# The eight modulation chunks of GpSimd moved to the weights' ring and TensorE

## Chip, cores and metric
The kernel runs on one core of one Trainium2 chip. The metric is the device time of one execution in microseconds (us).

## What is computed
Two blocks of two transformer layers each, on one sequence of 256 tokens of 1024 channels, all in float32. The first block's layers are modulated by a condition vector `c`; cut to what matters here:

```python
# first block, for each of 2 layers
mod = silu(c) @ ada_w[l] + ada_b[l]        # 1024 x 6144 weights, six vectors of 1024
sh_m, sc_m, gt_m, sh_f, sc_f, gt_f = split(mod, 6)
h = rms_norm(x, norm_mix) * (1 + sc_m) + sh_m
# o_a windowed attention, o_b compressed/selected attention, o_c gated delta net, all from h @ w_in
x = x + gt_m * (concatenate([o_a, o_b, o_c]) @ w_out)
h = rms_norm(x, norm_ffn) * (1 + sc_f) + sh_f
x = x + gt_f * ((silu(gate) * up) @ w_down)     # gate, up = h @ w_gate_up
```

The modulation vector of a layer is computed in 12 chunks of 512 columns, m = 0 to 11 for the first layer and 12 to 23 for the second. A chunk's weights are 1024 x 512, 2 MB. The second block (block attention with a learned choice of keys, dilated attention, and feed-forward layers with a short convolution) has no modulation. It uses a table of relative-position biases that the kernel widens in DRAM first (`bias_wide`, 6 MB).

## The kernel before
**Stages.** For each layer of the first block: `in` (five chunks of columns and one of tokens), `tok`, `cmp` (the compression network), attention, the gated delta net, `out` (two chunks), `gu` (gate and up, eleven chunks) and `dn` (down, eight tiles of 128 output channels). Layer numbers are added: gu0, dn0, gu1, dn1. Then the second block with `even`, `tail`, `o0`, `up0`, `down0`, `odd`, `o1`, `up1`, `down1`.

**Weights' ring.** All weights come through one ring of three slots (`SLOTS`). The order of the chunks is fixed when the program is built, by `phase` and `ada_chunks` (lines 98 to 122). SyncE (SP) issues the loads in that order; a load waits until the chunk three places ahead of it in the ring has been used (`load`, line 488): for weights of a matmul until TensorE has finished with it (`gemm_ready`), for an ada chunk until its sums have been copied out (`acc_ready`). SP runs its instructions in order, so a load that waits holds up everything behind it.

**Splitting.** A float32 product is made of three fp32r matmuls: high part by high, high by low, low by high. Each chunk is split in two halves. ScalarE copies a half to its high part (`high`, line 1111, a 2048-column copy, 1408 columns for down), and VectorE subtracts to get the low part (`low`, line 1483); GpSimd does this subtraction for the first three halves of `out` (line 1959). High parts are kept for three halves (`AHEAD`), so `high(u)` waits for TensorE to be done with half `u - 3`, and for a first half also for the chunk's landing.

**Modulation on TensorE.** 16 of the 24 chunks go through the ring. `ada_dots` (line 694) multiplies the chunk by silu(c) with eight 512-column matmuls into four row groups; ScalarE copies the rows out (`ada_rows`, line 1131); `modulations` (line 704) sums the four groups with four one-column matmuls into columns of PSUM bank 7. Chunks 0 to 3 come at the very start, 4 and 5 (16 and 17 in layer 1) inside `in`, the next two around `cmp` and attention, and two more in the delta net at inverse levels 1 and 3.

**Modulation on GpSimd.** The other eight, m = 10 to 15, 22 and 23, are loaded by GpSimd's own DMA queue into a part of the arena once the last mixer output is ready (`mix_ready`), multiplied by silu(c) and added up there (`weigh`, line 1967: one operation of 4096 columns, two of 2048 or 1024, one of 512). TensorE adds the partitions with the same `modulations`, ahead of gu and within it, and, for 12 to 15, ahead of tiles 1, 3, 5 and 7 of dn0. The modulations of m = 12 to 15 are read by VectorE in the last step of dn0's residual (line 1698).

**Delta net.** The inverse of a triangular matrix is built in seven levels. In a level TensorE makes T1 (line 821) for two halves of the heads, ScalarE copies each (line 1222), TensorE makes the two products dx (lines 829 and 831), VectorE updates X and XT (lines 1666 and 1668). GpSimd prepares the next level's mask (line 1993). ScalarE splits the first two halves of `out` ahead of level 1, the third after level 6 (`late_high`).

**End of a stage.** `norm_squares` (line 1080) squares the residual tile pairs as VectorE finishes them, with the `high` copies for the next stage in between; `norm_sums` sums on TensorE (line 690); ScalarE takes the root (line 1096), then one `high`, then `norm_high` writes the high part of the normalised tiles.

## Time and profile before

| | us |
|---|---|
| median of 3 timed runs | 1814.04 |
| lowest and highest | 1806.9, 1814.69 |
| profiled execution, own time | 1805.96 |
| its span from the first to the last instruction | 1804.2 |
| TensorE (PE) busy | 1608.9 |
| VectorE (DVE) busy | 1044.7 |
| ScalarE (ACT) busy | 784.3 |
| GpSimd (POOL) busy | 280.8 |
| mean granted TensorE clock, of full speed | 0.933 |

Busy times are unions of an engine's instructions and overlap between engines. Waits are inferred from semaphore events. PEclk is the granted TensorE clock as a share of the higher of its two levels, 2.4 GHz. Times inside the trace count from the span's start.

### The profile page before, as it was taken

The page shows a single profiled execution, that of the slowest core. Times are in us where ns is not written, and L with a number is a line of the kernel's source. Part 1 is how long each engine was busy: PE and PEld are TensorE (multiplying, and loading weights), DVE is VectorE, ACT ScalarE, POOL GpSimd, SP SyncE. Part 2 cuts the span into 40 slices and gives each one's busy share as a digit, 9 for nine tenths or more (in the row PEclk, how much of TensorE's full clock was granted, in tenths as well). Part 3 has the DMA queues.
Part 4 walks back from the last instruction along what each step waited for, and adds up shares of the span by engine and source line. Part 5 has one row for each costly group of instructions (what it writes and reads, how often), then busy time and mean ns, then how long its engine had stood idle before and what let it go on. Part 6 is the DMA issues. An engine that isn't in the chain of part 4 may idle for free.

```text
span 1804.2 us, 29358 instructions
## 1 busy us (share of the span) xinstructions
PE 1608.9 (89%) x12322; PEld 1510.8 (84%) x12322; DVE 1044.7 (58%) x1393; ACT 784.3 (43%) x1175; POOL 280.8 (16%) x102
## 2 busy tenths in 40 slices
PE   5899788899989997888999899569999998899997
PEld 2888478899988884788999799448999988789997
DVE  1573545886664735458554633685876454567853
ACT  3344423444343434234443443354664444556642
POOL 0000246663510002366000000220000000200000
PEclk7997799899999977998999899789999999999999
DMA  8365522565552551225544734202553545045442
GB/s 364 135 230 227 174 94 98 216 245 192 187 205 99 226 208 54 94 94 187 186 158 161 266 141 154 93 1 94 187 186 129 205 157 187 6 143 184 167 161 88
DMA packets 30191, 287.82 MB, mean 160 GB/s; under 512 B 2887, under 2 KB 11367, under 8 KB 11784
## 3 DMA queue, kind: packets, MB, share of 16 engines
q1 hardware_dynamic: 28888, 269.51, 40.7%
q0 software_dynamic: 1152, 16.78, 2.4%
q8 instruction: 79, 1.29, 0.3%
q14 instruction: 24, 0.20, 0.0%
q10 hardware_dynamic: 48, 0.05, 0.0%
HBM read 285.23 MB, written 7.39 MB: 162 GB/s over the span
## 4 chain that ended last, share of the span: by engine, by line
PE 73%; DVE 16%; ACT 3%; DMA 3%; issue 3%; POOL 1%; SPq 0%; POOLq 0%; DVEq 0%; ACTq 0%
PE bank L610 20%; PE bank L611 19%; PE bank L612 19%; DVE w_lo L1490 4%; DMA ring<-w_mix 2%; PE bank L992 2%; PE bank L690 2%; PE bank L748 2%; DVE arena L1804 2%; PE bank L831 1%; PE bank L736 1%; DVE lg L1516 1%; DVE h L1881 1%; PE bank L829 1%; ACT w_hi L1124 1%
## 5 line engine op out<-in xcount | busy, mean ns | idle before, releaser
L610 PE MATMUL bank<-hi_T,w_hi 128*128 128x256 f32 x2312 | 669.8, 290 | 35.1 <-DVE h_lo L1473 16.4
L612 PE MATMUL bank<-hi_T,w_lo 128*128 128x256 f32 x2312 | 664.3, 287 | 0.0
L1490 DVE TENSOR_TENSOR w_lo<-ring,w_hi 128x2048 fp32r<-128x2048 f32 (+2 forms) x218 | 508.9, 2345 | 228.7 <-ACT w_hi L1124 227.4
L611 PE MATMUL bank<-h_lo,w_hi 128*128 128x256 f32 x2056 | 590.8, 287 | 0.0
L1124 ACT ACTIVATE w_hi<-ring 128x2048 fp32r<-128x2048 f32 (+3 forms) x226 | 391.8, 1735 | 353.3 <-PE bank L612 280.3
L610 PEld LDWEIGHTS bank<-hi_T,w_hi 128*128 128x128 f32 x2312 | 455.2, 197 | 41.2 <-issue 33.1
L612 PEld LDWEIGHTS bank<-hi_T,w_lo 128*128 128x128 f32 x2312 | 454.6, 197 | 0.0
L611 PEld LDWEIGHTS bank<-h_lo,w_hi 128*128 128x128 f32 x2056 | 404.3, 197 | 0.4
L610 PE MATMUL bank<-act_hi,w_hi 128*128 128x256 f32 x704 | 201.5, 286 | 9.4 <-DVE act_lo L1503 7.7
L611 PE MATMUL bank<-act_lo,w_hi 128*128 128x256 f32 x704 | 200.5, 285 | 0.0
L612 PE MATMUL bank<-act_hi,w_lo 128*128 128x256 f32 x704 | 200.4, 285 | 0.0
L1953 POOL TENSOR_TENSOR lg<-lg,rec 128x512 f32<-128x512 f32 (+2 forms) x32 | 43.0, 1342 | 775.3 <-DVE rec L1532 734.0
L610 PEld LDWEIGHTS bank<-act_hi,w_hi 128*128 128x128 f32 x704 | 136.5, 194 | 10.3 <-DVE act_lo L1503 8.3
L611 PEld LDWEIGHTS bank<-act_lo,w_hi 128*128 128x128 f32 x704 | 136.6, 194 | 0.0
L612 PEld LDWEIGHTS bank<-act_hi,w_lo 128*128 128x128 f32 x704 | 136.4, 194 | 0.0
L1141 ACT ACTIVATE arena<-bank 128x256 f32<-128x256 f32 (+3 forms) x99 | 39.1, 405 | 152.0 <-PE bank L612 152.0
L1916 DVE SCALAR_TENSOR_TENSOR arena<-bank,v,arena 128x254 f32<-128x254 f32 (+1 forms) x176 | 72.9, 476 | 38.0 <-ACT arena L1426 37.8
L1964 POOL TENSOR_TENSOR w_lo<-ring,w_hi 128x2048 fp32r<-128x2048 f32 x8 | 36.0, 4531 | 298.9 <-ACT w_hi L1124 298.9
L1973 POOL TENSOR_TENSOR arena<-arena 128x2048 f32<-128x2048 f32 (+1 forms) x16 | 80.2, 5014 | 1.3
L1971 POOL TENSOR_TENSOR arena<-arena,c_silu 128x4096 f32<-128x4096 f32 x8 | 63.5, 7938 | 71.4 <-DMA arena<-ada 71.4
L611 PE MATMUL bank<-mix_lo,w_hi 128*128 128x256 f32 x256 | 73.9, 289 | 0.0
L610 PE MATMUL bank<-w_hi,hi_T 128*128 128x256 f32 (+2 forms) x240 | 68.1, 284 | 6.5 <-DVE w_lo L1490 6.5
(217 smaller groups left out, 2053.0 us busy)
## 6 DMA issues: line engine op xcount, KB each, us to landing
ring<-w_gu SPq DMA_DIRECT2D x22, 2048.0 KB, 8.2
ring<-w_dn SPq DMA_DIRECT2D x32, 1408.0 KB, 5.9
ring<-w_up SPq DMA_DIRECT2D x22, 2048.0 KB, 7.8
ring<-ada SPq DMA_DIRECT2D x16, 2048.0 KB, 7.4
ring<-w_mix SPq DMA_DIRECT2D x12, 2048.0 KB, 8.1
arena<-ada POOLq DMA_DIRECT2D x8, 2048.0 KB, 8.9
ring<-even_in SPq DMA_DIRECT2D x8, 2048.0 KB, 8.2
ring<-odd_in SPq DMA_DIRECT2D x6, 2048.0 KB, 7.8
```

Source lines behind the costliest of these rows:

```text
L610: nc.tensor.matmul(out, wh, xh, start=start, stop=False)
L611: nc.tensor.matmul(out, wh, xl, start=False, stop=False)
L612: return nc.tensor.matmul(out, wl, xh, start=False, stop=stop)
L690: last = nc.tensor.matmul(bank[:, 7, 0:S], const("ones"), h[:, k, :], start=(k == 0), stop=(k == KT - 1))
L748: last = nc.tensor.matmul(bank[0:HD, 6, lo * P:hi * P], v(kt), pT[0:n, u % 2, kt, lo * P:hi * P], start=U["start"] and kt == 0, stop=U["en ...
L1124: nc.scalar.activation(w_hi[:, u % AHEAD, 0:size], ring[:, slot, part * size:(part + 1) * size], ACT.Copy)\
L1141: nc.scalar.activation(dst, src, func).then_inc(gemm_freed, 1)
L1490: V.tensor_tensor(w_lo[:, n % SLOTS, at], ring[:, n % SLOTS, at], w_hi[:, u % AHEAD, 0:size].bitcast(F32), ALU.subtract).then_inc(w_lo_rea ...
L1916: V.scalar_tensor_tensor(out=cv[:, b, half, shift:S], in0=bank[:, 2 * b + half, 0:S - shift], scalar=cw[:, tap, at], in1=cv[:, b, half, sh ...
L1953: ins = G.tensor_tensor(out, out, along(rec[:, b, :], w), ALU.mult)
L1971: ch(G.tensor_tensor(ada_late, ada_late, along(c_silu, CH), ALU.mult))
L1973: ch(G.tensor_tensor(ada_late[:, 0:half], ada_late[:, 0:half], ada_late[:, half:2 * half], ALU.add))
```

## The change
All 24 chunks go through the ring and TensorE. In each layer six ada chunks instead of four stand between `cmp` and `out` in the ring, and the delta net takes one at each of the levels 1, 2, 3 and 4. The four for layer 1's start (12 to 15) come in dn0 behind tiles 0, 2, 4 and 6, dots and all; their modulations run between the tiles, the last one behind the last tile. ScalarE's row copies stand in `norm_squares` for dn0 between two `high` copies. The three `late_high` copies of `out` stand behind levels 3, 4 and 5. `weigh`, its buffers and its semaphore go. What follows is the diff, cut to its core.

```diff
-    NEXT_ADA = (1, 3, 5, 7)
+    NEXT_ADA = (0, 2, 4, 6)
...
         phase(f"cmp{l}", ["compress"] * 2)
-        ada_chunks(4)
+        ada_chunks(6)
         phase(f"out{l}", OUT)
         phase(f"gu{l}", UP)
-        phase(f"dn{l}", DOWN, FT * P // 2)
+        phase(f"dn{l}", DOWN, FT * P // 2, ada_after=() if l else NEXT_ADA)
...
# SyncE
                 load_phase(f"cmp{l}", w_cmp[l], 0, full)
-                for j in range(2, 6):
+                for j in range(2, 8):
                     load_ada(m + j)
                 if l == 0:
                     sp.dma_start(v2[:, :, :], vec2).then_inc(vec2_in, 16)
...
-                load_phase(f"dn{l}", w_dn[l], 2, FT * P)
+                for j, at in enumerate(phases[f"dn{l}"]["at"]):
+                    load(at, w_dn[l][j], FT * P)
+                    if l == 0 and j in NEXT_ADA:
+                        load_ada(ADA_L + NEXT_ADA.index(j))
...
# TensorE, delta_net
                 for lv in range(LEVELS):
-                    if lv == 3:
-                        modulations(m_next, m_next + 1)
+                    if lv in (3, 4):
+                        modulations(m_next + lv - 3, m_next + lv - 2)
                     pe.wait_ge(mb_ready, l * LEVELS + lv + 1)
-                    if lv in (1, 3):
-                        ada_dots(m_next + lv // 2)
+                    if 1 <= lv <= 4:
+                        pe.wait_ge(acc_ready, m_next + lv - 1)
+                        ada_dots(m_next + lv - 1)
...
-                modulations(m_next + 1, m_next + 2)
+                modulations(m_next + 2, m_next + 4)
...
# TensorE, down
-                    if name == "dn0" and j in NEXT_ADA:
-                        m = ADA_L + NEXT_ADA.index(j)
-                        if m == ADA_L:
-                            pe.wait_ge(mod_read, 2)
-                        modulations(m, m + 1)
...
                         last.then_inc(gemm_ready, 1)
+                    if name == "dn0" and j in NEXT_ADA:
+                        m = ADA_L + NEXT_ADA.index(j)
+                        if m == ADA_L:
+                            pe.wait_ge(mod_read, 2)
+                        else:
+                            modulations(m - 1, m)
+                        ada_dots(m)
+                if name == "dn0":
+                    modulations(ADA_L + ADA_FIRST - 1, ADA_L + ADA_FIRST)
...
# ScalarE, norm_squares
-                        for u in ahead if j < 3 else ahead[:-1]:
+                        for u in ahead[:-1]:
                             high(u)
+                        if norm_input[n] == "dn0":
+                            ada_rows(ADA_L + j)
+                        if j < 3:
+                            high(ahead[-1])
...
# ScalarE, delta_net
-                act.wait_ge(mb_ready, l * LEVELS + 1)
-                late_high(l, 0, 2)
                 for lv in range(1, LEVELS):
...
-                    if lv in (1, 3):
-                        ada_rows(m_next + lv // 2)
-                late_high(l, 2, AHEAD)
+                    if lv <= 4:
+                        ada_rows(m_next + lv - 1)
+                    if lv >= 3 and lv < 3 + AHEAD:
+                        late_high(l, lv - 3, lv - 2)
...
# GpSimd
-            def weigh(m):
-
-                pool.dma_start(ada_late, ada[m].rearrange("p (k n) -> p k n", k=KT)).then_inc(late_in, 16)
-                pool.wait_ge(late_in, 16 * (ada_alone.index(m) + 1))
-                ch(G.tensor_tensor(ada_late, ada_late, along(c_silu, CH), ALU.mult))
-                for half in (KT // 2, KT // 4):
-                    ch(G.tensor_tensor(ada_late[:, 0:half], ada_late[:, 0:half], ada_late[:, half:2 * half], ALU.add))
-                pool.wait_ge(mod_ready, m - 1)
-                G.tensor_tensor(late_sums[:, m % 2, :], ada_late[:, 0, :], ada_late[:, 1, :], ALU.add).then_inc(acc_ready, 1)
-                pool.wait_ge(acc_ready, m + 1)
```

The modulations ahead of gu and within it go as well (in the loop over layers and in `up`).

## Rows read from the trace of the kernel before

**Rows 1.** the page: busy us, share, instructions by engine; then the chain's shares.
```profile
PE 1608.9 (89%) x12322; PEld 1510.8 (84%) x12322; DVE 1044.7 (58%) x1393; ACT 784.3 (43%) x1175; POOL 280.8 (16%) x102
...
PE 73%; DVE 16%; ACT 3%; DMA 3%; issue 3%; POOL 1%; SPq 0%; POOLq 0%; DVEq 0%; ACTq 0%
```

**Rows 2.** timeline, out0: start, us, engine, line, operands, count, [idle before].
```profile
297.54 7.01 POOL L1971 TENSOR_TENSOR arena<-arena,c_silu 128x4096 f32<-128x4096 f32 x1 [7.52 <-DMA arena<-ada]
...
298.54 8.16 DVE L1490 TENSOR_TENSOR w_lo<-ring,w_hi 128x2048 fp32r<-128x2048 f32 x1 [1.46 <-ACT w_hi L1124]
...
329.22 2.29 DVE L1490 TENSOR_TENSOR w_lo<-ring,w_hi 128x2048 fp32r<-128x2048 f32 x1
```

**Rows 3.** timeline: norm sums and root after out0; norm sums after o0.
```profile
313.68 2.75 PE L690 MATMUL bank<-h,cn 128*128 128x256 f32 x12
...
320.59 0.47 ACT L1096 ACTIVATE std<-bank,cn 128x256 f32<-128x256 f32 x1 [1.41 <-PE bank L690]
...
1241.70 3.61 PE L690 MATMUL bank<-h,cn 128*128 128x256 f32 x16
```

**Rows 4.** timeline of the inverse levels, layer 0: ScalarE's copies, TensorE's ada work.
```profile
237.29 0.60 ACT L1222 ACTIVATE arena<-bank 128x512 f32<-128x512 f32 x1 [1.80 <-PE bank L821]
...
238.68 0.59 ACT L1136 ACTIVATE arena<-bank 128x512 f32<-128x512 f32 x1
...
242.71 0.60 ACT L1222 ACTIVATE arena<-bank 128x512 f32<-128x512 f32 x1 [3.44 <-PE bank L821]
...
251.66 0.60 ACT L1222 ACTIVATE arena<-bank 128x512 f32<-128x512 f32 x1 [6.71 <-PE bank L821]
...
257.07 0.60 ACT L1222 ACTIVATE arena<-bank 128x512 f32<-128x512 f32 x1 [3.44 <-PE bank L821]
...
263.19 0.60 ACT L1222 ACTIVATE arena<-bank 128x512 f32<-128x512 f32 x1 [3.87 <-PE bank L821]
...
269.30 0.60 ACT L1222 ACTIVATE arena<-bank 128x512 f32<-128x512 f32 x1 [3.87 <-PE bank L821]
...
247.73 0.95 PE L714 MATMUL bank<-cn,arena 128*128 128x1 f32 x8
...
248.61 1.92 PE L700 MATMUL bank<-ring,c_wide 128*32 128x512 f32 x16
```

**Rows 5.** DMA issues, 168 to 210 (last: landing time); stretch 178 to 203.
```profile
bias_wide<-bias_dram SPq DMA_DIRECT2D x1, 6144.0 KB, 31.9
...
ring<-w_out SPq DMA_DIRECT2D x1, 2048.0 KB, 28.5
...
178.00:203.00 25.00, 19.77 (x94) 11.88 (x94) 18.68 (x34) 13.22 (x55) 5.80 (x8) 0.80 0.95 300
```

**Rows 6.** stretches: length, busy us (count) by engine, clock, DMA share, GB/s.
```profile
339.10:458.95 119.85, 117.14 (x969) 116.19 (x968) 94.71 (x49) 52.10 (x52) 65.63 (x17) 1.00 0.58 217
...
837.30:953.26 115.96, 115.96 (x969) 115.95 (x968) 66.59 (x51) 52.14 (x52) 11.71 (x3) 1.00 0.47 170
...
458.95:532.36 73.41, 68.84 (x561) 68.46 (x561) 43.37 (x30) 25.35 (x20) 24.78 (x7) 0.98 0.55 205
...
953.26:1016.69 63.43, 63.43 (x529) 63.39 (x528) 28.35 (x25) 25.25 (x20) 0.00 (x0) 1.00 0.56 204
```

**Rows 7.** a stretch shortly after dn0's first wait.
```profile
466.80:470.20 3.40, 3.40 (x18) 3.40 (x18) 0.00 (x0) 0.00 (x0) 0.00 (x0) 0.50 0.00 0
```

**Rows 8.** the page's DMA issues: count, KB each, median us from issue to landing.
```profile
ring<-w_dn SPq DMA_DIRECT2D x32, 1408.0 KB, 5.9
...
ring<-ada SPq DMA_DIRECT2D x16, 2048.0 KB, 7.4
```

**Rows 9.** timeline at the turn from gu1 to dn1.
```profile
953.32 1.38 ACT L1124 ACTIVATE w_hi<-ring 128x1408 fp32r<-128x1408 f32 x1 [2.56 <-PE bank L612]
...
956.28 0.68 DVE L1503 TENSOR_TENSOR act_lo<-arena,act_hi 128x512 fp32r<-128x512 f32 x1
```

**Rows 10.** timeline: ScalarE's first normalised tiles of in1.
```profile
538.74 1.30 ACT L1108 ACTIVATE hi_T<-h,mod 128x256 fp32r<-128x256 f32 x3 [0.61 <-DVE h L1455]
```

More of the change, by code:

```diff
@@ L117, in ada_chunks @@
         for _ in range(n):
-            if late_ada(len(ada_at)):
-                ada_at.extend([None] * (2 + ADA_FIRST))
             ada_at.append(count["chunk"])
@@ L122, in ada_chunks @@
             count["chunk"] += 1
-    def late_ada(m):
-        return ADA_L - 2 <= m < ADA_L + ADA_FIRST or m >= ADA - 2
-    NEXT_ADA = (1, 3, 5, 7)
+    NEXT_ADA = (0, 2, 4, 6)
     IN_ADA = (2, 4)
@@ L148, in hybrid_then_mixture @@
     phase("down1", DOWN, FT * P // 2)
-    ada_at.extend([None] * 2)
-    ada_alone = [m for m in range(ADA) if ada_at[m] is None]
-    on_pe = [m for m in range(ADA) if ada_at[m] is not None]
     def ada_bank(m):
         i = m % ADA_L
-        return i + 2 if i < ADA_FIRST else 2 if i == ADA_FIRST + 2 else 6
+        return i + 2 * (m < ADA_L) if i < ADA_FIRST else 2 if i == ADA_FIRST + 2 else 6
     late = [u for l in range(L1) for u in range(phases[f"out{l}"]["u0"], phases[f"out{l}"]["u0"] + AHEAD)]
@@ L189, in hybrid_then_mixture @@
         c_in = sb("c_in", [P, KT])
-        c_silu = sb("c_silu", [P, KT])
         c_wide = sb("c_wide", [P, KT, 32])
@@ L273, in hybrid_then_mixture @@
         acc = view(18432, 2, CH)
-        ada_late = view(19008, KT, CH)
-        late_sums = pT[:, :, 0, :]
         qk2 = view(0, 25, S)
@@ L323, in hybrid_then_mixture @@
         mod_ready = sem("mod_ready")
-        late_in = sem("late_in")
         mod_read = sem("mod_read")
@@ L709, in modulations @@
                         at = MOD_COL + 4 * m + t
-                        if ada_at[m] is not None:
-                            sums_m, ones = acc[:, m % 2, :], const("pick")[:, 0:1]
-                        else:
-                            sums_m, ones = late_sums[:, m % 2, :], const("ones")[:, 0:1]
-                        last = nc.tensor.matmul(bank[:, 7, at:at + 1], sums_m[:, t * P:t * P + P], ones,
-                                                start=True, stop=True)
+                        last = nc.tensor.matmul(bank[:, 7, at:at + 1], acc[:, m % 2, t * P:t * P + P],
+                                                const("pick")[:, 0:1], start=True, stop=True)
                     last.then_inc(mod_ready, 1)
@@ L873, in projection, with up @@
                     columns_chunk(name, nn, 4 * nn, (hi_T, mix_lo), ready)
-            def up(name, first, m_next=None):
+            def up(name, first):
                 ph = phases[name]
@@ L897, in up @@
                 for j in range(SLOTS * turns, 11):
-                    if m_next and j == SLOTS * turns:
-                        modulations(m_next, m_next + 1)
                     one(j, u0 + 2 * j + 1, t0 + 4 * j - 3)
@@ L1016, in _ @@
                 pe.wait_ge(std_ready, n + 2)
-                modulations(m + 6, m + 7)
-                up(f"gu{l}", norm_end[n + 1] - KT, m + 7)
+                up(f"gu{l}", norm_end[n + 1] - KT)
                 down(f"dn{l}", 11 * (l + 1))
@@ L1131, in ada_rows @@
             def ada_rows(m):
-                act.wait_ge(rows_ready, on_pe.index(m) + 1)
+                act.wait_ge(rows_ready, m + 1)
                 if m >= 2:
@@ L1264, in _ @@
             act.wait_ge(c_loaded, 16)
-            nc.scalar.activation(c_wide[:, :, :], along(c_in[:, :], 32), ACT.Silu)
-            nc.scalar.activation(c_silu[:, :], c_in[:, :], ACT.Silu).then_inc(c_ready, 1)
+            nc.scalar.activation(c_wide[:, :, :], along(c_in[:, :], 32), ACT.Silu).then_inc(c_ready, 1)
             act.wait_ge(tab_ready, 1)
@@ L1965, in low @@
                                 ALU.subtract).then_inc(w_lo_ready, 1)
-            def weigh(m):
-                pool.dma_start(ada_late, ada[m].rearrange("p (k n) -> p k n", k=KT)).then_inc(late_in, 16)
-                pool.wait_ge(late_in, 16 * (ada_alone.index(m) + 1))
-                ch(G.tensor_tensor(ada_late, ada_late, along(c_silu, CH), ALU.mult))
-                for half in (KT // 2, KT // 4):
-                    ch(G.tensor_tensor(ada_late[:, 0:half], ada_late[:, 0:half], ada_late[:, half:2 * half], ALU.add))
-                pool.wait_ge(mod_ready, m - 1)
-                G.tensor_tensor(late_sums[:, m % 2, :], ada_late[:, 0, :], ada_late[:, 1, :], ALU.add).then_inc(acc_ready, 1)
-                pool.wait_ge(acc_ready, m + 1)
-            pool.wait_ge(c_ready, 1)
             for l in range(L1):
@@ L1996, in _ @@
                     low(u)
-                pool.wait_ge(mix_ready, 3 * (l + 1))
-                for m in ada_alone[(2 + ADA_FIRST) * l:(2 + ADA_FIRST) * (l + 1)]:
-                    weigh(m)
             pool.wait_ge(w_lo_ready, phases["o0"]["u0"] + 1)
```

## The prediction
> **What bounds the kernel now.** I read the engine shares and the chain first. TensorE is busy 89% of the span and holds 73% of the chain, so time is won where TensorE waits and lost where it gets more to do or waits anew; GpSimd's 281 us matter only through what they hold up [rows 1]. What they hold up shows on VectorE's rows at the end of out0: one half-chunk subtraction (`low`) takes 8.16 us there against 2.29 us later. It began 1 us after GpSimd's first weighing multiplication (297.54 to 304.55) and ended at 306.70, one plain duration after it [rows 2]. Then I read TensorE's stretches by stage, the inverse levels on ScalarE's copies, and last the landing times of the SP queue, since the change moves loads.
>
> The sum is made against the profiled execution (span 1804.2, own time 1805.96 us). The three timed runs have the median 1814.04, 8 us above it.
>
> **Gains: the weighing goes.**
> (a) End of out0: TensorE starts the norm sums at 313.68, but the last four wait for squares that wait for stretched `low`s, and the standard deviation is taken at 320.59. Where no GpSimd work is near, 16 such matmuls run on in 3.61 us [rows 3]. So std would come at 313.7+3.6 = 317.3: 3.3 us saved. Layer 1 shows the same picture once, 3.0 us. Together -6.3.
> (b) gu0 against gu1, ten chunks each between the same issues: 119.85 and 115.96 us [rows 6]. The difference is waits behind stretched DVE work: -3.9. Each of the two stretches also holds one modulation (four one-column matmuls and their weight loads, 0.95 us as a group, some 0.8 once the pipeline overlaps) which moves into the delta net: -1.6. Together -5.5.
> (c) The modulation before gu goes too; it lay in the wait for the normalised tiles, so 0. GpSimd's own DMA queue goes; nobody waited on it but GpSimd: 0.
>
> **Costs in the inverse levels, both layers.** ScalarE's first T1 copy marks each level: 237.29, 242.71, 251.66, 257.07, 263.19, 269.30 [rows 4]. A plain level is 6.1 us. Dots and a modulation ahead of level 3 make that step 8.95, and the next is 5.4, because both halves are then ready. So dots with modulation cost 2.85-0.7 = 2.1, and dots alone (1.92 us on TensorE) 1.2. The change adds dots at level 2 and dots with modulation at level 4: +3.35 a layer. ScalarE's row copies (0.6) and the `late_high` of 1.9 after levels 3, 4, 5 fit in its gaps as long as the chunk is there. The second modulation after the output matmuls (0.8) lies in the wait for `on_ready`; uncovered it would cost 0.8 a layer.
>
> **The load that ends up in the way (layer 0).** SP is one queue in program order. Today `bias_wide` (6 MB, DRAM to DRAM) is issued after the ada load that waits for the sums of m = 6, in the attention stage. In the new order two more ada loads stand ahead of it, and the last, m = 11, waits for the sums of m = 8: ScalarE's copy at 238.68 to 239.27, inside level 1 [rows 4]. So `bias_wide` goes out at about 240, and w_out's first chunk, which now waits for the sums of m = 9 (level 2, about 246.5), behind it. What such a place in the queue costs is on record: the w_out chunk issued behind `bias_wide` today needed 28.5 us to land, and the 16 DMA engines moved 300 GB/s for the 25 us in which that copy ran (178 to 203) [rows 5]. Harmless there: the levels only begin after 230, and nothing on ScalarE waits for it before. Now: ada 11 issued 239.3, landed +7.4 = 246.7 [rows 8]; `bias_wide` 25 us, to 271.7; w_out's own 2 MB at least 5 us more (7.4 less the start), 277.1. But `late_high(l, 0, 1)` stands in ScalarE's program after level 3, ahead of the T1 copies of level 4, and it waits for that chunk. Queued behind it on ScalarE: T1 copies of level 4, sums of m = 11, all that follows; TensorE waits for the copies. Copy of the half 1.9: level 4's T1 copy at 279.1 instead of 261.1; level 5 +5.4, level 6 +6.1 = 290.6 against 269.30 now: +21.3. TensorE stands still some 16 us before; after a wait of 2.8 us it was granted half its clock (0.50, the 1.2 GHz level) for a stretch [rows 7], and the dx matmuls are what a level consists of, so I add 3 (bounds 0 and 7). Layer 0: +24.3. Bounds from the rows: if the bias copy did not hold w_out at all, +3.35; if w_out needed its full 28.5 us after the bias issue plus ada 11, 4 more than taken. I take the middle mechanism because the 28.5 us row is this very pair of transfers. Layer 1 has no such copy: +3.35.
>
> The Trainium skill bears on this ("DMA: Bandwidth & Descriptors", Queues, rings and completion order): on each DMA engine the descriptors of one issuing queue are consumed in ring order. By that rule w_out waits out the whole bias copy, total about +30; if instead transfers of one queue shared the engines evenly, w_out would land near 262, and the total would be about +11. The trace's 28.5 us agree with the rule.
> For (a) and (b), "SBUF — State Buffer", Who interferes with whom, says that a DVE operation with two SBUF inputs is shut out for the whole of a GpSimd instruction that reads SBUF; the 8.16 us row agrees, and without GpSimd the whole stretch is returned. No other sum comes from it.
>
> **dn0.** Undisturbed, dn1 takes 63.43 us; dn0 takes 73.41 now, with four modulations, a 2.8 us wait for act_lo, and others [rows 6]. New: 63.43 + four dots of 1.9 (7.5) + three modulations between tiles (2.5) = 73.4, so the work alone makes up for what goes. Then the ring. (i) ada 12 takes the slot after w0, so w1 waits for gu's last chunk (t = 0), lands at +5.9 [rows 8], and ScalarE's gate chunk 10 has `high` of w1's first half ahead of `hidden_high(10)`. In dn1 these steps run at +0.06 to +3.70 (`high` starts 953.32, act_lo ends 956.96, last issue 953.26) [rows 9]; all start 5.9 later: act_lo at +9.6, while TensorE wants it at half a tile, +3.96. Wait 5.6, and half clock after it, 2. (bounds 0 and 3.4.) (ii) w3, w5, w7 wait for the odd tile before (T), with an ada load issued at T-1.9 (ScalarE's rows copy comes after `high` of the same half). Landed: T-1.9+7.4+3.3 = T+8.8, `high` 1.38, `low` 1.6: T+11.8; TensorE is there at T+7.9+0.8+1.9 = T+10.6. Wait 1.2, three times: 3.6 (bounds 0 and 9). dn0 = 73.4+5.6+2+3.6 = 84.6: +11.2.
>
> **dn0 to in1.** The last modulation comes after the last tile and after ScalarE's row copy, and VectorE's `modulation(1)` and gain, then the last residual, behind it: about +2.1 on std. Then `high(ahead[-1])` needs in1's second chunk; its load waits for the sums of m = 15 (end of dn0 +0.5), lands +7.4, copy 1.9: +9.8, and `norm_high` stands behind it on ScalarE. Now hi_T starts at 538.74, 6.4 after dn0's end at 532.36 [rows 10]. The two overlap: +3.4 in all (bounds 2.1 and 4.5).
>
> **Sum.** -6.3 -5.5 +24.3 +3.35 +11.2 +3.4 = +30. On the profiled execution 1836, on the median 1844; as the timed runs spread from 1806.9 to 1814.7, I forecast 1842.
>
> **Rivals.**
> 1. The bias copy does not hold w_out (shares the engines evenly). For it: 300 GB/s is a mean over 25 us, and w_out's packets may well slip in between. Against: the 28.5 us. Then layer 0 costs about 5 instead of 24: +11, 1825. Chance 0.10.
> 2. Not slower: loads are hidden everywhere. w_out's chunk lands before level 4's copies want it, w1 within 4 us of gu's end, in1's second chunk before std. It decides at one point, whether SP gets past ada 11 and the bias copy before level 3 ends (about 255). Then only -6.3-5.5+3.35+3.35+0 (dn0) +1.4 (last modulation) = -3.7: 1810. For it: DMA runs at 0.5 to 0.6 of its time in gu and dn. Against: the order on SP. Chance 0.08.
> 3. Waits feed the clock: after the 16 us stand TensorE stays at the low level into the solve (+7), dn0's odd tiles wait 3 instead of 1.2 (+5), +42: 1856. For it: every idle stretch here is followed by PEclk 0.5. Against: levels keep TensorE busy otherwise. Chance 0.12.
> The forecast has 0.70.
>
> Range for 8 in 10: 1820 to 1857, from rival 1 to rival 3; the forecast's own range is 1832 to 1852. What one can tell from no change is about 0.5% (9 us). Slower by more: forecast, rival 3, and half of rival 1: 0.87. Within: half of rival 1 and most of rival 2: 0.10. Faster: 0.03.
>
> **What the new profile would show.** Right: a wait of ScalarE's `w_hi` copy for DMA of w_out of 15 to 22 us in layer 0 and none in layer 1; GpSimd's busy time far below 281 us; `low` at 2.29 in out0; ada dots about level 2 and 4; a wait for act_lo of 5 to 6 us at dn0's start; hi_T of in1 about 10 us after dn0. Wrong: bias_wide landing before 250, or level 4's copies at 261; gu0 still slower than gu1; dn0 at 74.

## The result and the profile after

| | us, median (range), runs |
|---|---|
| before | 1812.49 (1806.90 to 1814.69), 4 |
| after | 1839.22 (1832.64 to 1840.31), 4 |
| ratio | 1.0145, 95% interval 1.0111 to 1.0179 |

The kernel became 26.7 us slower between the medians; the forecast was 1842, 28 to 30 us slower. The profiled execution took 1839.05 us with a span of 1837.3, which is 33.1 us more than the span before (the execution profiled before was a low one of its runs, the one profiled now is not). The comparison of traces below is against these 33.1.

The page after, in the form of [rows 1]: busy time and the chain's shares.

```profile
PE 1629.5 (89%) x12450; PEld 1519.1 (83%) x12450; DVE 965.4 (53%) x1393; ACT 787.0 (43%) x1182; POOL 113.3 (6%) x62
...
PE 75%; DVE 12%; DMA 7%; ACT 3%; issue 2%; POOL 1%; POOLq 0%; SPq 0%; DVEq 0%; ACTq 0%
```

GpSimd lost 167.5 us of work and VectorE 79 us of stretching, as the change meant. TensorE gained 20.6 us. What ate the gain stands in the chain: DMA went from 3% to 7% of it. A shift at a time, measured between the same events of both traces (start of the group named to start of the next; the end of level 0 is taken at TensorE's first T1 product of layer 0 and at ScalarE's first T1 copy of level 1 in layer 1):

| stretch | forecast, us | measured, us |
|---|---|---|
| start to the end of level 0, layer 0 | 0 | +0.4 |
| inverse levels and what follows, to out0's first product | +24.3 | +23.8 |
| out0 to its root | -3.3 | -2.3 |
| gu0, to dn0's first product | -4.7 | -5.9 |
| dn0 and the turn to in1's first `hi_T` | +14.6 | +19.7 |
| in1 to the end of level 0, layer 1 | 0 | -1.9 |
| inverse levels of layer 1 | +3.35 | +3.65 |
| out1 to its root | -3.0 | -3.3 |
| gu1, dn1 | -0.8 | -1.4 |
| the rest | 0 | +0.4 |
| sum | +30.4 | +33.1 |

**Levels of layer 0.** ScalarE's timeline over the levels (L1211 copies T1, L1115 splits a weight, L1127 copies an ada chunk's rows); compare [rows 4].

```profile
238.90 0.60 ACT L1211 ACTIVATE arena<-bank 128x512 f32<-128x512 f32 x1 [12.56 <-PE bank L807]
...
246.37 0.60 ACT L1211 ACTIVATE arena<-bank 128x512 f32<-128x512 f32 x1 [5.49 <-PE bank L807]
...
254.62 0.60 ACT L1211 ACTIVATE arena<-bank 128x512 f32<-128x512 f32 x1 [6.28 <-PE bank L807]
...
277.80 1.91 ACT L1115 ACTIVATE w_hi<-ring 128x2048 fp32r<-128x2048 f32 x1 [21.20 <-DMA ring<-w_out]
279.62 1.07 ACT L1211 ACTIVATE arena<-bank 128x512 f32<-128x512 f32 x2
...
287.22 0.60 ACT L1211 ACTIVATE arena<-bank 128x512 f32<-128x512 f32 x1 [4.25 <-PE bank L807]
...
293.33 0.60 ACT L1211 ACTIVATE arena<-bank 128x512 f32<-128x512 f32 x1 [2.07 <-PE bank L807]
```

Between levels 3 and 4 lie 25.0 us where there were 5.4, and the bracket names the reason: the split of out0's first half, which stands in ScalarE's program between the two, waited 21.20 us for its load. The T1 copies of level 4 were queued behind it. SP's queue shows why the load was late (start, time taken at the queue, the load issued), and the DMA views how long it took (KB each, median us from issue to landing; the copy from the view of 235 to 290, out0's first load alone from the view of 248 to 250):

```profile
168.37 72.86 SPq L479 DMA_DIRECT2D ring<-ada  x4
...
241.75 0.62 SPq L535 DMA_DIRECT2D bias_wide<-bias_dram  x1
248.37 13.91 SPq L479 DMA_DIRECT2D ring<-w_out  x2
```

```profile
bias_wide<-bias_dram SPq DMA_DIRECT2D x1, 6144.0 KB, 31.1
ring<-w_out SPq DMA_DIRECT2D x1, 2048.0 KB, 29.4
```

SP passed the last ada load at 241.2 and sent the 6 MB copy at 241.75 (about 240 in the forecast). w_out went out at 248.37 behind it and was there at 277.8 (277.1 in the forecast), 4.9 us after the copy (241.75 + 31.1 = 272.9). In the kernel before, the load behind the copy also landed 4.9 us after it (203.5 and 208.4, [rows 5] with the issue times 171.59 and 179.91). TensorE stood still for 16.5 us:

```profile
PE bank L815 <- ACT arena L1211: 16.5, 1, 16.5
```

The step from level 4 to level 5, which begins at a granted clock of 0.50, took 7.6 us where experiment 1 below has 5.4. Another 1.2 us of the +23.8 lie before level 1's copies: from 231.5 to 237.5 the mean clock was 0.72, against 1.00 in the kernel before. Experiment 1 has the same 0.72 there and the three runs of experiment 5, with the same program up to there, have 1.00, so these 1.2 us are no price of the change.

**out0.** `low` beside no GpSimd work is 2.29 us, where [rows 2] has 8.16, and the sixteen norm sums run on as one group, as after o0. The rows are VectorE's, TensorE's and ScalarE's of one stretch of the timeline; compare [rows 3].

```profile
323.69 2.29 DVE L1479 TENSOR_TENSOR w_lo<-ring,w_hi 128x2048 fp32r<-128x2048 f32 x1 [1.46 <-ACT w_hi L1115]
...
338.82 3.61 PE L679 MATMUL bank<-h,cn 128*128 128x256 f32 x16
...
342.48 0.47 ACT L1087 ACTIVATE std<-bank,cn 128x256 f32<-128x256 f32 x1 [2.31 <-PE bank L679]
```

**Stretches.** Windows by length, busy us (count) of PE, PEld, DVE, ACT, POOL, granted clock, DMA share and GB/s, as [rows 6]: gu0, dn0, gu1 of the changed kernel, then two stretches at a clock of 0.50, behind the end of the levels and in dn0, as [rows 7].

```profile
359.93:474.96 115.03, 115.03 (x961) 115.03 (x960) 58.90 (x50) 52.03 (x52) 0.00 (x0) 1.00 0.48 177
474.96:566.45 91.49, 79.28 (x619) 73.03 (x617) 28.62 (x25) 26.57 (x24) 0.00 (x0) 0.93 0.54 205
870.96:986.01 115.05, 115.05 (x961) 115.05 (x960) 58.92 (x50) 52.02 (x52) 0.00 (x0) 1.00 0.47 171
...
312.20:319.03 6.83, 5.95 (x28) 5.95 (x29) 1.27 (x4) 0.10 (x1) 0.00 (x0) 0.50 0.00 0
482.90:486.30 3.40, 1.74 (x8) 1.75 (x9) 1.68 (x3) 1.13 (x1) 0.00 (x0) 0.50 0.00 0
```

gu0 now equals gu1, TensorE busy without a gap, 4.8 us shorter than before; gu1 is 0.9 shorter, which is its one modulation. dn0 went from 73.41 to 91.49, of which TensorE stood still 12.2 us (4.6 before). What it waited for in 470 to 570 (us in total, times, longest):

```profile
PE bank L599 <- DVE w_lo L1479: 6.5, 3, 2.6
PE bank L599 <- DVE act_lo L1492: 5.7, 1, 5.7
```

and how the first of the odd tiles' waits comes about, on TensorE (dots L689) and ScalarE:

```profile
490.95 1.92 PE L689 MATMUL bank<-ring,c_wide 128*32 128x512 f32 x16
...
513.98 0.55 PE L599 MATMUL bank<-act_hi,w_hi 128*128 128x256 f32 x1 [2.44 <-DVE w_lo L1479]
...
499.45 0.57 ACT L1127 ACTIVATE arena<-bank 128x512 f32<-128x512 f32 x1
510.80 1.38 ACT L1115 ACTIVATE w_hi<-ring 128x1408 fp32r<-128x1408 f32 x1 [10.78 <-DMA ring<-w_dn]
```

The dots end at 492.87, but ScalarE copies their rows at 499.45, behind the third of the splits that it makes ahead. The next ada load waits for that copy and goes out at 500.05, one us before the load of w3, so that both are under way at once: 9.8 us from issue to split, where the page has a median of 5.8 for w_dn. The loads of w5 and w7 went out 2.1 us behind an ada load and took 8.8 and 9.9.

### The profile page after: what moved, and what is told of

Read it like the earlier page. It is cut to its first block, busy times and chain, and to the rows that moved or that the text cites. A ratio compares the mean times of both kernels' runs of the same rounds, so it can differ in the third digit from the quotient of the medians.

```text
span 1837.3 us, 29587 instructions
## 1 busy us (share of the span) xinstructions
PE 1629.5 (89%) x12450; PEld 1519.1 (83%) x12450; DVE 965.4 (53%) x1393; ACT 787.0 (43%) x1182; POOL 113.3 (6%) x62
## 4 chain that ended last, share of the span: by engine, by line
PE 75%; DVE 12%; DMA 7%; ACT 3%; issue 2%; POOL 1%; POOLq 0%; SPq 0%; DVEq 0%; ACTq 0%
PE bank L599 20%; PE bank L600 20%; PE bank L601 20%; DMA ring<-w_mix 2%; PE bank L980 2%; PE bank L679 2%; DMA ring<-w_dn 2%; PE bank L733 2%; DMA ring<-w_out 2%; PE bank L689 2%; DVE arena L1793 1%; DVE w_lo L1479 1%; PE bank L817 1%; PE bank L721 1%; PE bank L807 1%
## 5 line engine op out<-in xcount | busy, mean ns | idle before, releaser
L1479 DVE TENSOR_TENSOR w_lo<-ring,w_hi 128x2048 fp32r<-128x2048 f32 (+2 forms) x218 | 447.7, 2062 | 295.9 <-ACT w_hi L1115 294.4
L1115 ACT ACTIVATE w_hi<-ring 128x2048 fp32r<-128x2048 f32 (+3 forms) x226 | 391.7, 1734 | 399.8 <-PE bank L601 263.4
L599 PEld LDWEIGHTS bank<-act_hi,w_hi 128*128 128x128 f32 x704 | 138.2, 196 | 21.2 <-DVE act_lo L1492 11.2
L600 PE MATMUL bank<-w_lo,hi_T 128*128 128x256 f32 (+2 forms) x240 | 68.3, 285 | 0.0
L601 PE MATMUL bank<-w_hi,h_lo 128*128 128x256 f32 (+2 forms) x240 | 68.3, 284 | 0.0
L689 PE MATMUL bank<-ring,c_wide 128*32 128x512 f32 x384 | 57.7, 727 | 9.3 <-DMA ring<-ada 8.9
```

The lines of the kernel that those rows point to most:

```text
L599: nc.tensor.matmul(out, wh, xh, start=start, stop=False)
L600: nc.tensor.matmul(out, wh, xl, start=False, stop=False)
L601: return nc.tensor.matmul(out, wl, xh, start=False, stop=stop)
L689: last = nc.tensor.matmul(bank[rows, ada_bank(m), :], c_wide[:, k, :], w[:, k, :], start=k < 4, stop=k >= 4, tile_position=(0, 32 * (k % 4)))
L1115: nc.scalar.activation(w_hi[:, u % AHEAD, 0:size], ring[:, slot, part * size:(part + 1) * size], ACT.Copy)\
L1479: V.tensor_tensor(w_lo[:, n % SLOTS, at], ring[:, n % SLOTS, at], w_hi[:, u % AHEAD, 0:size].bitcast(F32), ALU.subtract).then_inc(w_lo_rea ...
```

## Experiments

Each kernel is the changed one with the edit shown. Ratios are to the kernel before, on the same chip, with the 95% interval. The kernel before had a median of 1811.17 beside experiments 1 to 4, of 1809.58 beside experiment 5 and the run "early rows, last early", and of 1812.74 beside the other runs of experiment 6 and "again". So a difference between runs of different groups is given by the medians and, where it matters, by the ratios too.

### 1. The bias copy ahead of the added loads

```diff
-                for j in range(2, 8):
+                for j in range(2, 6):
                     load_ada(m + j)
...  # v2 and bias_wide, layer 0
+                for j in range(6, 8):
+                    load_ada(m + j)
```

> The copy of bias_wide is issued ahead of the two ring loads that the change added (modulations 6 and 7 of layer 0), not behind them. Theory: the layer-0 levels grew by 23.8 us because the copy now lies ahead of w_out in its DMA queue, so that ScalarE's split of w_out waits 21.2 us; the dots, splits and transposes themselves cost about what they cost in layer 1 (3.65 us). Then the split of w_out waits for nothing long, the levels of layer 0 take about 3.5 us more than in the kernel before, and the time falls by 20 us, to about 1819. Rival, that the growth of layer 0's levels is the added work of the engines (the copies of hi_T and lo_T, the dots, the splits of the two modulations) and the wait would be hidden by it: under 5 us, 1835 to 1839.

Measured: 1822.55, ratio 1.0066 (1.0044 to 1.0088): 16.7 below the changed kernel's median, 14 by the ratios. The trace's stretch of the levels is 4.6 us over before, not 23.8; 1.2 of the 4.6 are the clock of 0.72 named above. ScalarE's timeline there (L1117 is the split, L1213 T1's copy), then SP's queue:

```profile
255.07 0.60 ACT L1213 ACTIVATE arena<-bank 128x512 f32<-128x512 f32 x1 [6.28 <-PE bank L809]
...
257.56 1.91 ACT L1117 ACTIVATE w_hi<-ring 128x2048 fp32r<-128x2048 f32 x1 [0.51 <-DMA ring<-w_out]
263.33 0.60 ACT L1213 ACTIVATE arena<-bank 128x512 f32<-128x512 f32 x1 [3.86 <-PE bank L809]
...
268.75 0.60 ACT L1213 ACTIVATE arena<-bank 128x512 f32<-128x512 f32 x1 [1.64 <-PE bank L809]
```

```profile
173.92 0.62 SPq L535 DMA_DIRECT2D bias_wide<-bias_dram  x1
```

The split waited 0.51 us instead of 21.20. The copy itself was no faster: the ada load that now stands behind it took 29.5 us, but nothing waited for it.

```profile
ring<-ada SPq DMA_DIRECT2D x1, 2048.0 KB, 29.5
```

The cost of the levels but the work itself was this one order in SP's queue. So the rival (work of the engines) falls. The time fell by less than the 20 us expected: the levels gave 19.1, but gu0 and the stretch from in1 to layer 1's levels came out 1.2 and 1.3 longer than in the changed kernel's trace, for no reason that the traces show. out0 keeps its whole gain: 3.3 us below before, the figure of the forecast, where the changed kernel had 2.3. dn0 with its turn took 100.5 us, against 101.0 in the changed kernel: the two places are independent.

### 2. GpSimd's work put back, for nothing

```diff
+            def weigh(i, m):
+                pool.dma_start(ada_late, ada[m]...[:, 0:KT - 1]).then_inc(late_in, 16)
+                pool.wait_ge(late_in, 16 * (i + 1))
+                ch(G.tensor_tensor(ada_late, ada_late, along(c_in[:, 0:KT - 1], CH), ALU.mult))
...  # added up in four steps
+                pool.wait_ge(mix_ready, 3 * (l + 1))
+                for i, m in enumerate((10, 11, 12, 13, 14, 15, 22, 23)[6 * l:6 * l + 6]):
+                    weigh(6 * l + i, m)
```

> As the run with the early bias copy, and GpSimd again loads seven of the eight rows of each of the eight modulations into a buffer of its own, weighs and adds them, with the operations and element counts of the kernel before; the result is used by nobody. Theory: GpSimd's weighing holds up VectorE's splits (the split of a weight beside it took 8.16 us against 2.29 alone) and the gate's first levels of work, so this run gives back what the change gained at out0, out1 and gu0: 10 to 15 us more than the run with the early copy, about 1831. Rival, that the gains of out0 and gu0 come from the removed wait for GpSimd's result alone and not from the work beside VectorE: under 3 us more than that run.

Measured: 1832.16, ratio 1.0110 (1.0074 to 1.0147): 9.6 above experiment 1 by the medians, 8 by the ratios, just under the theory's range. (The weighing here leaves out one of the eight rows, so its large operations are an eighth or a quarter shorter than before's.) Stretch by stretch against experiment 1: out0 to its root +1.3, gu0 to dn0's first product +5.7, dn0 with its turn +5.8, out1 to its root +1.2; the rest, mostly stretches without this work, is 5.4 shorter. The splits on VectorE in 290 to 425, first here, then in experiment 1 (us in total, mean ns of one):

```profile
L1489 DVE TENSOR_TENSOR w_lo<-ring,w_hi 128x2048 fp32r<-128x2048 f32 x19 | 75.0, 3949 | 7.8 <-ACT w_hi L1122 7.7
```

```profile
L1481 DVE TENSOR_TENSOR w_lo<-ring,w_hi 128x2048 fp32r<-128x2048 f32 x20 | 45.8, 2292 | 26.3 <-ACT w_hi L1117 26.3
```

The gains at gu0 come from the work beside VectorE, since nobody reads this result: the rival falls there. The loads of GpSimd's own queue came back as well, but from out0 to the end of gu0 ScalarE waited for no load of the ring in this run, so they are not what held up the splits. At out0 the work gave back only 1.3 of 3.3: the first split beside it took 6.52 us here and 8.16 before [rows 2], so this run, with its shorter operations, does not price that term fully. Both splits end 2.15 us after the GpSimd multiplication that they began beside (309.70 after 307.55 here, 306.70 after 304.55 before), nearly the 2.29 that such a split takes alone:

```profile
301.39 6.16 POOL L1970 TENSOR_TENSOR arena<-arena,c_in 128x3584 f32<-128x3584 f32 x1 [6.72 <-DMA arena<-ada]
...
303.18 6.52 DVE L1489 TENSOR_TENSOR w_lo<-ring,w_hi 128x2048 fp32r<-128x2048 f32 x1 [1.46 <-ACT w_hi L1122]
```

The 5.8 us in dn0 have no counterpart in the forecast: the last of the six weighings of layer 0 runs to 477, over the end of gu0 and the start of dn0, and the wait for act_lo grew from 5.9 to 9.4: the split ahead of it took 4.30 us instead of 1.62. The Trainium skill ("SBUF — State Buffer", Who interferes with whom) says that a VectorE instruction with two SBUF inputs contends with a GpSimd instruction that reads SBUF, and calls the ports that they share an exclusive lock. The two ends at 2.15 us after the GpSimd instruction agree.

### 3. dn0: the modulations one tile later

```diff
-    NEXT_ADA = (0, 2, 4, 6)
+    NEXT_ADA = (1, 3, 5, 6)
```

> The four modulations between down tiles stand behind tiles 1, 3, 5 and 6 instead of behind 0, 2, 4 and 6, in both layers; the bias copy stays as the change has it. Theory: at the head of dn0 the first modulation's split stands on ScalarE between the last product of the gate and the first split of the down weights, and its products between w0 and w1 on TensorE; one tile later they leave the start of dn0 alone, so the wait of w1 for act_lo (5.7 us) and the half clock behind it (about 3 us) go: 6 to 9 us less, about 1832. Rival, that the wait only moves to the next odd tile, because the ring is what is late: within 3 us of 1839.

(The edit touches dn0 alone; dn1 has no modulations. "Both layers" in the text above is a slip.) Measured: 1825.25, ratio 1.0079 (1.0054 to 1.0104): 14.0 below the changed kernel by the medians, 12 by the ratios, against the 6 to 9 expected. dn0 took 75.07 us (first product to last). The `act_lo` wait went, as the theory has it, but so did the odd tiles' waits, of which 0.9 us were left. The theory was right on the place and wrong on the extent: this edit removes two causes and not one, which the next runs separate.

### 4. dn0: ScalarE's row copy two splits earlier

```diff
-                        for u in ahead[:-1]:
+                        for i, u in enumerate(ahead[:-1]):
                             high(u)
-                        if norm_input[n] == "dn0":
-                            ada_rows(ADA_L + j)
+                            if i == 0 and norm_input[n] == "dn0":
+                                ada_rows(ADA_L + j)
```

> Ahead of dn0's norm, ScalarE splits the modulation right behind the first of the three tiles that it splits ahead, instead of behind all three; the bias copy stays as the change has it. Theory: the ring loads behind that modulation are issued some 9 us earlier, so that the three waits of the odd tiles w3, w5 and w7 for their splits (2.6, 2.4 and 1.5 us by the starts of their products) and most of dn0's stretches at half clock go; 6 to 10 us less, about 1831. Rival, that dn0's growth of 18 us over before is the added dots, copies and splits on engines that would be late anyway: within 2 us of 1839.

Measured: 1832.34, ratio 1.0124 (1.0085 to 1.0163): 6.9 below the changed kernel by the medians, within the theory's range, but 4 by the ratios, whose intervals overlap: by the timed runs alone this gain is not shown. The trace is plainer: dn0 took 82.71 us instead of 91.69 (first product to last), and of its waits only act_lo's was left. ScalarE's timeline and TensorE's waits in dn0:

```profile
495.16 0.60 ACT L1127 ACTIVATE arena<-bank 128x512 f32<-128x512 f32 x1 [9.33 <-PE bank L689]
...
508.90 1.38 ACT L1115 ACTIVATE w_hi<-ring 128x1408 fp32r<-128x1408 f32 x1 [6.87 <-DMA ring<-w_dn]
```

```profile
PE bank L599 <- DVE act_lo L1492: 5.7, 1, 5.7
```

The rows are copied 0.1 us after the dots end and no longer 6.6 us. The next ada load leaves at 495.78, 7.4 us ahead of w3's (503.22), and w3 is split 5.7 us after its issue instead of 9.8.

### 5. Two at a time

The early bias copy with the tiles 1, 3, 5, 6:

> Both edits together: the copy of bias_wide ahead of the two added ring loads, and the four modulations of dn0 behind tiles 1, 3, 5 and 6. Theory: two places that don't touch each other, w_out's wait in the delta net (16 us) and the waits at dn0 (14 us by the run of e3_tiles), so the gains add up: about 1809, the time of the kernel before within its spread. Rival, that loads moved forward by the one come to wait at the other, or that the clock gives part back: 1814 or more.

the same with the early row copy:

> As e5_bias_tiles, and ScalarE's split of the modulation stands behind the first of the three tiles that it splits ahead in dn0's norm. Theory: with the tiles 1, 3, 5 and 6 the ring is ahead already (one wait of 0.9 us for a split of the down weights is left in dn0), so this edit is worth nothing more: within 2 us of e5_bias_tiles. Rival, that the 7 us that it gave alone are of another kind than those of the tiles: 4 or more below.

and the early bias copy with only the first modulation moved (tiles 1, 2, 4, 6):

> The early bias copy, and of dn0's modulations only the first moved, from behind tile 0 to behind tile 1; the others stay behind 2, 4 and 6. It tells the two waits of dn0 apart, the one for act_lo at its start and those of the odd tiles for their splits. Theory: each is there on its own account, so this run keeps the odd tiles' waits: act_lo's wait of 5.7 us and the half clock behind it go, 7 to 9 less than with the early copy alone, 1814 to 1816, and two or three waits for w_lo stay. Rival, that the odd tiles' waits are the lateness of the first load carried on through the ring: all of it goes, as in e5_bias_tiles, about 1809.

| run | us | ratio (interval) | dn0 | turn to in1 |
|---|---|---|---|---|
| bias, tiles 1 3 5 6 | 1806.71 | 0.9988 (0.9970 to 1.0007) | 74.86 | 11.57 |
| the same kernel again | 1805.72 | 0.9956 (0.9941 to 0.9970) | 75.14 | 11.79 |
| bias, tiles 1 3 5 6, rows early | 1822.00 | 1.0049 (1.0031 to 1.0068) | 89.85 | 9.36 |
| bias, tiles 1 2 4 6 | 1809.01 | 0.9991 (0.9972 to 1.0010) | 79.98 | 9.27 |

(In the tables "dn0" is from its first product to the end of its last, "turn" from there to in1's first product, in the profiled execution.)

The first pair of gains adds up: 15.8 us below experiment 1, 32.5 below the changed kernel. The second expectation failed, and on the side that neither theory had: the early row copy, which with tiles 0, 2, 4, 6 takes 9.0 us from dn0, adds 15.0 to it with 1, 3, 5, 6 (15 by the medians too, 11 by the ratios). Its ScalarE and TensorE timelines:

```profile
472.35 0.60 ACT L1129 ACTIVATE arena<-bank 128x512 f32<-128x512 f32 x1 [12.46 <-PE bank L691]
472.85 2.63 ACT L1117 ACTIVATE w_hi<-ring 128x1408 fp32r<-128x1408 f32 x2
...
475.93 0.39 PE L601 MATMUL bank<-act_hi,w_hi 128*128 128x256 f32 x1 [3.64 <-DVE w_lo L1481]
```

and TensorE's waits in dn0, here, then with the tiles 1, 3, 5, 6 alone, then with 1, 2, 4, 6:

```profile
PE bank L601 <- DVE w_lo L1481: 11.1, 3, 3.7
```

```profile
PE bank L601 <- DVE w_lo L1481: 0.7, 1, 0.7
```

```profile
PE bank L601 <- DVE w_lo L1481: 5.7, 3, 2.6
```

ScalarE stood 12.46 us at the row copy of dots that come a whole tile later, with two splits for TensorE's next tile queued behind it. So one rule fits all of dn0's orders that were run. In step j ScalarE makes four splits, of which the first waits for TensorE to be done with half 4j, the second with 4j+1, the third with 4j+2 and the fourth with 4j+3 (in the last step the fourth stands behind the root). The orders without a long wait for w_lo have the row copy behind the split that waits for the first half of the very tile behind which the dots stand: with the dots behind tile 2j that is the first split, with tile 2j+1 the third. (Only the last step of 1, 3, 5, 6 is out of place, and behind it no more loads of dn0 are issued.) The second and the fourth were not tried. The changed kernel has the copy behind the third and the dots behind tile 2j: that split can't begin before the next half is done, and the rows are copied 6.6 us late. In the run above the copy is two splits too early instead.

The last of the three separates the two waits at dn0. With only the first modulation moved, `act_lo`'s 5.9 us of wait are gone and three waits for w_lo stay, 5.7 us in total (8.1 in experiment 1, 6.5 in the changed kernel): they are for the most part not lateness carried on from the start, and the rival falls on the trace. By the timed runs it looks otherwise: 13.5 us below experiment 1, not 7 to 9, and only 2.3 above the version with all four moved. Three things make that up. The waits that stay are 2.4 us shorter. They are followed by no stretch at half clock (the mean clock of dn0 is 1.00; 0.91 from 445 to 500 in experiment 1). And of the 5.1 us that dn0 is shorter with 1, 3, 5, 6, the turn takes 2.3 back: there the last row copy stands behind a split that waits 4.26 us for in1's first chunk, and ends with the last tile (530.28 against 529.99) instead of 1.5 us ahead of it, and the root comes 7.4 us behind dn0's end instead of 5.1. A wait moved rather than went.

### 6. Each row copy in its place, and the last modulation

Tiles 1, 2, 4, 6, the first row copy behind the third split, the other three behind the first:

```diff
+                            if i == (0 if j else 2) and norm_input[n] == "dn0":
+                                ada_rows(ADA_L + j)
```

> The early bias copy, the modulations of dn0 behind tiles 1, 2, 4 and 6, and ScalarE's split of each put where its rows are ready: the first behind the third split ahead, the other three behind the first split ahead. Theory from the runs before: what counts at dn0 is that ScalarE's copy of the rows stands right behind the split that waits for the same products. Half a tile later it delays the next ring load by 8 us (the waits of 5.7 us for w_lo in e7_first_tile); half a tile earlier it holds up two splits (11.1 us in e6_bias_rows_tiles). Here every one of them is matched, so e7_first_tile's three waits go and the short turn to in1 stays: 3 to 6 us below e7_first_tile, 1803 to 1806, at or a little below the kernel before. Rival, that the waits only move to the turn (which is 2.3 us longer in e5_bias_tiles than in e7_first_tile): within 2 us of e7_first_tile and e5_bias_tiles, 1807 to 1809.

The last modulation between the halves of the last tile, on top of that and, before it, on top of the version with the early rows:

```diff
                         last.then_inc(gemm_ready, 1)
+                        if name == "dn0" and u == ph["u1"] - 2:
+                            modulations(ADA_L + ADA_FIRST - 1, ADA_L + ADA_FIRST)
```

> As e6_bias_rows_tiles, and the four one-column products of dn0's last modulation run between the two halves of the last tile instead of behind it. Theory: behind the last tile they hold up VectorE's modulation, gain and last residual, and with them the next norm, so they cost 1 to 2 us: that much below e6_bias_rows_tiles. Rival, that the turn from dn0 to the next stage waits for the load of its second chunk anyway: no difference.

> As e9_order, and the products of dn0's last modulation between the two halves of the last tile. Theory: the last residual and the norm then don't wait for them; e8_last_early was 1.4 us shorter than e6_bias_rows_tiles from gu0's eighth chunk to dn0's std, so 1 to 2 us below e9_order. Rival, that the turn to in1 ends on a load: no difference.

> The kernel of e5_bias_tiles once more, beside the two others on one chip: 0.9988 of the kernel before, by its first measurement; e9_order is expected 2 to 3 us below it by the one theory and equal to it by the other.

| run | us | ratio (interval) | dn0 | turn | sum |
|---|---|---|---|---|---|
| rows in place | 1805.24 | 0.9961 (0.9944 to 0.9978) | 75.62 | 9.65 | 85.27 |
| the same, last early | 1804.29 | 0.9951 (0.9931 to 0.9970) | 76.59 | 8.66 | 85.25 |
| early rows, last early | 1818.36 | 1.0047 (1.0028 to 1.0065) | 89.05 | 8.76 | 97.81 |

The windows of dn0 and of the turn, for the version with rows in place:

```profile
455.58:531.20 75.62, 74.20 (x621) 68.19 (x619) 27.24 (x25) 26.08 (x24) 0.00 (x0) 1.00 0.73 278
531.20:540.85 9.65, 4.51 (x26) 3.70 (x24) 7.84 (x12) 6.25 (x8) 0.00 (x0) 0.96 0.65 248
```

and for tiles 1, 3, 5, 6:

```profile
455.13:529.99 74.86, 74.19 (x618) 67.99 (x616) 28.19 (x25) 26.43 (x24) 0.00 (x0) 1.00 0.67 257
529.99:541.56 11.57, 6.46 (x26) 5.14 (x25) 6.98 (x12) 5.89 (x8) 0.00 (x0) 0.85 0.91 360
```

Putting the copies in place takes 4.0 us from dn0 and its turn against tiles 1, 2, 4, 6 alone (89.25 to 85.27), as the matching theory has it. Two of the three waits for w_lo went; one of 1.4 us stayed, where the theory had none:

```profile
PE bank L601 <- DVE w_lo L1481: 1.4, 1, 1.4
```

Against tiles 1, 3, 5, 6 it is 1.2 us in the trace, and on one chip the medians, 1805.24 and 1805.72, can't be told apart: here the rival's time came out. Moving the last modulation is 1.4 us in the trace in the pair with early rows (99.21 to 97.81) and 0.0 in the other; by the medians 3.6 and 1.0, by the ratios 0.0002 and 0.0010. No gain of it is shown.

The three versions measured side by side (rows in place, the same with the last modulation early, and tiles 1, 3, 5, 6 again) are faster than the kernel before on that chip, the best by 0.5% (0.3 to 0.7%). The first measurement of tiles 1, 3, 5, 6, on another chip, was level (0.9988, an interval that takes in 1). So the idea of the change can win, by 7 to 9 us on one chip, with no win shown on the other; 35 us of the changed kernel were the order of a few instructions.

## Why the prediction was right

**The load in the way: right, step by step.** The issue of the copy (about 240; 241.75), w_out's landing (277.1; 277.8), ScalarE's wait (15 to 22; 21.2) and the level's sum (+24.3; +23.8) came as worked out, and moving that one issue took back 19.1 us. The half clock behind the standstill was put at 3 us and was 2.2. This rests on the 28.5 us of [rows 5], the same pair of transfers in the same order. The Trainium skill ("DMA: Bandwidth & Descriptors", Queues, rings and completion order) says that each DMA engine takes the descriptors of one ring in order; the 29.4 us that w_out took behind the copy, against 8.7 in experiment 1, agree. Rival 1 (+11) falls.

**The work in the levels: right.** +3.35 a layer; 3.65 in layer 1, and 3.65 in layer 0 too in the run with the bias copy early and tiles 1, 3, 5, 6. It is the price that no reordering removes.

**The gains: right in sum.** Forecast -11.8, measured -12.9 (-2.3, -5.9, -3.3, -1.4). The 1 us missing at out0 goes with a stretch at a clock of 0.50 that is 6.8 us long at its start (rows above) where the kernel before has 3.4. The levels' standstill did not leave it there: the clock was 1.00 from 284.9 to 312.2, and experiment 4, which keeps the standstill, has 3.4 us of half clock there and 3.6 us less than before from out0 to its root (its windows):

```profile
315.00:318.40 3.40, 3.14 (x14) 3.15 (x15) 0.46 (x3) 0.00 (x0) 0.00 (x0) 0.50 0.00 0
318.40:325.00 6.60, 6.60 (x57) 6.60 (x57) 1.35 (x3) 2.33 (x2) 0.00 (x0) 1.00 0.01 2
```

In gu0 the stall term (-3.9) is what the stretch between the issues behind chunks 0 and 7 lost (84.4 to 80.5); 0.9 went behind it, with the modulation that stood there, and 1.1 ahead of it, which the working had at nothing. In gu1 it is 0.9 for the modulation (forecast 0.8) and 0.5 ahead of it.

**dn0: the mechanisms right, one term too small.** Forecast 84.6, measured 91.5. The work (73.4) fits the 74.9 of a version with one wait of 0.7. act_lo's wait was 5.6 in the forecast, 5.7 in the trace. The term that was mis-sized is "three ring waits of 1.2": they were 2.4, 1.5 and 2.6, in all 6.5 against 3.6. w5 came as worked out (landed T+8.8, T being the end of the tile before). w3 landed at T+9.8 (T = 501.00), because its ada load had left only 0.95 us ahead of T, not 1.9; w7 landed at T+9.9 though its ada load had the time assumed, since the two loads under way together took longer than the 3.3 us allowed. The sum lies within the bounds given (0 and 9), but the value taken was at the low side. And the clock was counted once, at the start (2), though it fell behind two of the odd tiles' waits as well: w3 and w4 took 17.4 us together and w7 9.6, where undisturbed ones take 16.1 and 8.2, so 2.8 us more. The forecast took the row copy's place for a given. It named it in passing ("ScalarE's rows copy comes after `high` of the same half"), but did not see it as the cause: with the copy two splits earlier the three waits are gone.

**The turn: too large.** +3.4 forecast, +1.6 measured: the first `hi_T` came 8.0 us behind dn0's end, not about 10. Of the two terms taken to overlap only one showed: in1's second chunk was there 0.4 us after the root, so the modulation behind the last tile was nearly all.

**What made the total fit.** dn0 with its turn was 5.1 us too low; against it stand 1.9 us less in in1 and 1.1 more gained than forecast. The 1.9 is not explained: the stretch from in1's `hi_T` to out1 ranges from 249.1 to 251.8 us between the profiled executions of the runs with the same code there. That these errors partly cancelled is luck, and so is part of the fit of 1842: the sum was 2.7 us under the +33.1 between the traces, and the execution profiled before was a low one, so the medians lie only 26.7 apart.

Rival 2 (not slower) named the point from which it decides: whether SP gets past the last ada load and the bias copy before level 3 ends. Experiment 1 makes that true and nothing else, and the loss of the levels shrinks to their work. Its other half, w1 in time at dn0, needed the other edit. With both the kernel is at 1806, near the 1810 that the rival gave for this case. Rival 3 falls: TensorE was back at the full clock at 284.9, well before the solve. Its ground, that every idle stretch is followed by a clock of 0.50, does not hold either: behind the wait of 1.76 us at 498.7 in the kernel before, the clock stayed at 1.00.

```profile
498.70:502.10 3.40, 3.40 (x28) 3.40 (x29) 3.40 (x2) 0.63 (x1) 3.32 (x2) 1.00 0.90 370
```

## What to carry to other kernels

A load that waits on a queue read in program order carries everything behind it along: before adding one, look for the large transfer that stands behind it, and where its successor is first needed. When work is moved by a tile on one engine, the instruction on the other engine that answers to it has to be moved by the same tile; the early place took 9 us from dn0 in one order of the tiles and added 15 in the other. And a wait found at the start of a stage does not explain the waits further on: move the first alone and see what stays.

## What the runs showed that was not expected

- After six of the seven waits of TensorE of 3.4 to 3.7 us inside otherwise gapless products of dn0 the next ones ran at half clock for 2.8 to 3.4 us (in the run with early rows and tiles 1, 3, 5, 6 after each of its three waits, 1.4 us lost each time). After the seventh, 3.64 us in the same kernel with the last modulation early, they did not (the wait and the window behind it are below). After waits of 2.4 and 2.6 us they ran at half clock in the changed kernel, while after 2.6 us in the run with tiles 1, 2, 4, 6 and one of about 2.6 in experiment 1 they did not. So the loss behind a short wait can't be had from the length of the wait alone.

```profile
477.51 0.39 PE L601 MATMUL bank<-act_hi,w_hi 128*128 128x256 f32 x1 [3.64 <-DVE w_lo L1481]
...
477.50:480.90 3.40, 3.39 (x28) 3.39 (x29) 3.40 (x3) 1.90 (x2) 0.00 (x0) 1.00 0.96 410
```

- The same four dots and four row copies, put in six orders, make dn0 from 74.9 to 91.7 us long.
